# A hybrid decoder step on one core: v projected ahead of the sample requests' attention, layer norm of the gate moved between the samples

## The reference

```python
h = rmsnorm(x, norm_mix)
q_b, k_b, v_b, z_u, z_v, q_c, gate_logits = split(h @ w_in, IN_SPLITS)
u = gelu(z_u); v = layernorm(gelu(z_v), ln_v_g, ln_v_b)
A = u * (W_s v + b)                      # causal 128x128, four channel groups
B = dilated window attention(q_b, k_b, v_b)   # sample rows: keys and values of a cache plus their own
C = attention(q_c, memory)               # sample rows: a cached memory
x = x + (sig(g_A)*P_A(A) + sig(g_B)*P_B(B) + sig(g_C)*P_C(C)) @ w_out
x = x + MoE(rmsnorm(x))                  # top 4 of 32 experts, clamped SwiGLU
y = rmsnorm(x)
```

## Time and profile before

| | |
|---|---|
| median of three runs | 1395.66 us (1394.77 to 1399.48) |
| the profiled execution | 1399.48 us, span 1397.70 us |
| TensorE busy | 1324.9 us, 95% of the span |
| VectorE busy | 371.7 us, 27% |
| ScalarE busy | 249.1 us, 18% |
| mean granted TensorE clock | 0.984 of full |
| chain that ended last | TensorE 59%, DMA 35%, VectorE 3% |

### The profile page before, as it was taken

One profiled execution on the slowest core, in us unless ns is written; L12 is line 12 of the kernel. 1 busy time (PEld: TensorE's weight loads), 2 busy tenths in 40 slices (PEclk: granted clock), 3 DMA queues, 4 the chain that ended last, 5 costly groups with the idle time before them and its releaser, 6 DMA issues.

```text
span 1397.7 us, 19052 instructions
## 1 busy us (share of the span) xinstructions
PE 1324.9 (95%) x7749; PEld 634.9 (45%) x7749; DVE 371.7 (27%) x832; ACT 249.1 (18%) x406; POOL 60.2 (4%) x101
## 2 busy tenths in 40 slices
PE   6999889969996999999999999999999999999997
PEld 5675477637753333433343333333334333343333
DVE  2105654211316222212221222212222122221223
ACT  2011122210214211111121112111111111121112
POOL 2031401110000000000000000000000000000000
PEclk9999999989998999999999999999999999999999
DMA  9998876477873899999999999999999999999994
GB/s 339 374 347 300 281 261 218 158 228 269 314 318 139 310 430 429 429 429 429 428 429 428 428 429 429 429 428 430 429 428 428 428 429 430 428 429 429 429 427 174
DMA packets 56939, 515.13 MB, mean 369 GB/s; under 512 B 5379, under 2 KB 6491, under 8 KB 31536
## 3 DMA queue, kind: packets, MB, share of 16 engines
q1 hardware_dynamic: 50000, 493.68, 86.0%
q0 software_dynamic: 6576, 20.25, 4.5%
q10 hardware_dynamic: 336, 0.82, 0.2%
HBM read 511.21 MB, written 47.52 MB: 400 GB/s over the span
## 4 chain that ended last, share of the span: by engine, by line
PE 59%; DMA 35%; DVE 3%; issue 1%; ACT 1%; POOL 0%; SPq 0%; DVEq 0%; ACTq 0%
PE psum L567 56%; DMA weights<-in_w_gate_up 34%; PE psum L570 2%; DMA weights<-in_w_mem_kv 1%; DMA weights<-in_cache_mem_kv 1%; DVE qk L1387 1%; DVE pair L1233 0%; ACT th L1556 0%; DVE x L1415 0%; POOL weights L510 0%; DVE kvt L1279 0%; DVE kc L1292 0%; DVE va L1110 0%; DVE va L1111 0%; DVE va L1109 0%
## 5 line engine op out<-in xcount | busy, mean ns | idle before, releaser
L567 PE MATMUL psum<-weights,wsp 128*64 128x512 f32 x2048 | 487.5, 602 | 12.4 <-DMA weights<-in_w_gate_up 11.1
L567 PE MATMUL psum<-weights,merged 128*64 128x512 f32 (+2 forms) x1152 | 272.8, 595 | 1.5 <-issue 1.5
L567 PEld LDWEIGHTS psum<-weights,wsp 128*64 128x64 f32 x2048 | 129.3, 136 | 255.5 <-issue 202.6
L1358 DVE TENSOR_TENSOR hT<-psum,hT 128x264 f32<-128x264 f32 x256 | 98.8, 428 | 515.0 <-PE psum L567 515.0
L567 PE MATMUL psum<-hT,weights 128*128 128x264 f32 x704 | 164.3, 391 | 1.2 <-DVE pair L1233 0.9
L567 PEld LDWEIGHTS psum<-weights,merged 128*64 128x64 f32 (+2 forms) x1152 | 89.6, 140 | 156.3 <-issue 154.6
L567 PEld LDWEIGHTS psum<-hT,weights 128*128 128x128 f32 x704 | 133.7, 192 | 28.6 <-DVE pair L1233 4.6
L1617 ACT COPY bT<-psum 128x264 f32<-128x264 f32 x33 | 12.5, 380 | 476.6 <-PE psum L570 476.5
L567 PE MATMUL psum<-bT,merged 64*128 64x264 f32 x512 | 91.6, 435 | 0.0
L1387 DVE TENSOR_SCALAR qk<-psum,lowest 128x512 f32<-128x512 f32 x64 | 48.0, 751 | 158.3 <-PE psum L567 154.8
L567 PEld LDWEIGHTS psum<-bT,merged 64*128 64x128 f32 x512 | 38.5, 184 | 103.8 <-issue 103.8
(11 more groups left out here) (270 smaller groups left out, 727.4 us busy)
## 6 DMA issues: line engine op xcount, KB each, us to landing
weights<-in_w_gate_up SPq DMA_DIRECT2D x128, 2048.0 KB, 24.6
weights<-in_w_down SPq DMA_DIRECT2D x64, 2048.0 KB, 22.9
out<-in_cache_win_kv SPq DMA_DIRECT2D x8, 4094.0 KB, 20.7
weights<-in_w_in SPq DMA_DIRECT2D x13, 2048.0 KB, 12.4
out<-in_cache_win_kv SPq DMA_DIRECT2D x2, 4088.0 KB, 19.4
weights<-in_cache_mem_kv POOLq DMA_DIRECT2D x14, 512.0 KB, 7.4
weights<-in_cache_win_kv POOLq DMA_DIRECT2D x42, 128.0 KB, 5.7
weights<-in_w_mem_kv SPq DMA_DIRECT2D x2, 2048.0 KB, 17.8
```

What stands on the lines that cost most here:

```text
L567: return nc.tensor.matmul(out, lhsT, rhs, start=start, stop=stop, **kw)
L1358: V.tensor_tensor(acc[:, c, :], p_a[j % 2][part], acc[:, c, :], ALU.add).then_inc(s_acc, 1)
```

## The change

In the list, all of v (prompt and samples) is projected right after k, then come all six kt, then qc. zv 0 moves between qcs and qrest, vts ahead of qlow. Between the samples stand now zvs, zv 1, zvz and the four zu. norm_v moves from behind sdot 6 to behind sdot 3; vat and sp come ahead of sdot 6. The weight blocks of v are loaded ahead of qc's, with `LAST_USE` to match. On POOL the twelve outputs of keys and values are issued ahead of keys(3) instead of behind keys(7).

```diff
-    out += [("qc", cols(w_in, CO, CO + 512)), ("v0", cols(w_in, VO, VO + 512)), ("v1", cols(w_in, VO + 512, VO + 768))]
-    out += [("zv", cols(w_in, ZO, ZO + 512)), ("zu", cols(w_in, UO, UO + 512))]
+    out += [("v0", cols(w_in, VO, VO + 512)), ("v1", cols(w_in, VO + 512, VO + 768))]
+    out += [("qc", cols(w_in, CO, CO + 512)), ("zv", cols(w_in, ZO, ZO + 512)), ("zu", cols(w_in, UO, UO + 512))]
...
-    s += [("kt", 2, 0), ("kt", 2, 1)] + [("qc", m) for m in range(4)]
-    s += [("qs", 0), ("qs", 1), ("qcs",), ("vs", 0), ("qrest",), ("v", 0, 0), ("qlow",), ("kt", 0, 0), ("kt", 0, 1), ("selfb",)]
-    s += [("skb", 0), ("skc", 0), ("skb", 1), ("kt", 1, 0), ("kt", 1, 1), ("vsz", 0)]
-    fill = {2: [("v", 1, 0)], 3: [("vs", 1), ("v", 0, 1)], 4: [("vsz", 1), ("v", 1, 1)], 5: [("zv", 0)], 6: [("zvs",), ("vts",)], 7: [("zv", 1)]}
+    s += [("vs", 0), ("v", 0, 0), ("vsz", 0), ("v", 1, 0), ("vs", 1), ("v", 0, 1), ("vsz", 1), ("v", 1, 1)]
+    s += [("kt", t, n) for t in range(3) for n in range(2)] + [("qc", m) for m in range(4)]
+    s += [("qs", 0), ("qs", 1), ("qcs",), ("zv", 0), ("qrest",), ("vts",), ("qlow",), ("selfb",)]
+    big = [("zvs",), ("zv", 1), ("zvz",)] + [("zu", m) for m in range(4)]
+    s += [("skb", 0), ("skc", 0), ("skb", 1)]
     for b in range(2, NS):
-        s += fill[b] + [("skc", b - 1), ("skb", b), ("sdot", b - 2)]
-    s += [("zvz",), ("zu", 0), ("zu", 1), ("sdot", NS - 2), ("norm_v",), ("skc", NS - 1), ("zu", 2), ("zu", 3), ("vat",)]
-    s += [("sp", 0), ("sp", 1), ("sp", 2), ("sp", 3), ("sdot", NS - 1), ("p", "a", 0), ("g", "a", 0), ("slog",)]
+        s += {2: big[0:2], 3: big[2:4], 7: []}.get(b, big[b:b + 1]) + [("skc", b - 1), ("skb", b), ("sdot", b - 2)]
+        if b == 5:
+            s += [("norm_v",)]
+    s += [("vat",), ("sp", 0), ("sp", 1), ("sp", 2), ("sp", 3), ("sdot", NS - 2), ("p", "a", 0), ("skc", NS - 1), ("sdot", NS - 1), ("g", "a", 0), ("slog",)]
...
-LAST_USE = {("kc", 3): 0, ("vc", 1): 1, ("q", 3): 2, ("k", 1): 3, ("k", 5): 4, ("qc", 3): 5, ("v", 1, 0): 6, ("v", 1, 1): 7,
+LAST_USE = {("kc", 3): 0, ("vc", 1): 1, ("q", 3): 2, ("k", 1): 3, ("k", 5): 4, ("v", 1, 0): 5, ("v", 1, 1): 6, ("qc", 3): 7,
...
-            for b in range(KEYS, NS):
-                keys(b)
             taken(pool, "v", 1, 1)
             taken(pool, "vsz", 0)
             taken(pool, "vsz", 1)
-            taken(pool, "kt", 1, 1)
+            taken(pool, "kt", 2, 1)
...
+            for b in range(KEYS, NS):
+                keys(b)
             for b in range(ROUND):
                 values(b)
```

## The result

The changed kernel takes **1409.68 us** (median of 4 runs, 1407.23 to 1411.33), the kernel before beside it 1396.02 (1394.77 to 1399.48): ratio 1.0092, 95% interval 1.007 to 1.0113. The forecast was 1407.5, with 1401 to 1413 as range. The profiled execution took 1409.84 us, its span is 1408.0.

A forecast was written before the change was run, and what follows sets the result against it. It took the mixer ahead of the DMA-bound experts to pass delays one for one, with VectorE's list setting the changed stretch: 9.0 us of waits plus 2.9 of clock, 11.9 on the median 1395.66, gives 1407.5; range 1401 to 1413.

The forecast's parts named there:

- step 6: Clock loss behind new TensorE waits: 1.7 us at zvs and zv 1, 0.5 at skb 7 and vat, 0.7 at "p" and "g".
- Steps 1 and 2: TensorE up to skb 0: eight groups move ahead, done at 150.9, then a 2.6 us wait to 153.5.
- step 2: ScalarE waits for zv 0's Gelu before casting q, then VectorE's qlow; TensorE idles 2.6 us ahead of skb 0.
- Step 3: sdot 0 to 3: skc 1 behind zvs and zv 1 makes sdot 2 2.9 us later, zvz and a zu 0.6.
- The signs to watch for: Expected after: TensorE waits of 2 to 3, some 8 and 4 us, VectorE without long gaps 154 to 209, score at 211 to 215.
- Steps 4 and 5: Layer norm behind sdot 3 takes 9.9 us, TensorE waits some 8, then 4 more; second score 9.0 later before clock loss.
- (a): Rival: TensorE is the limit, its waits and clock loss go, 11.6 us faster, 1384.1; chance 0.06.
- Step 7: POOL and SP: moved outputs, key landings and weight blocks cost nothing, with 3 us as bound for late keys.
- (b): Rival: no change, as the DMA-bound expert stage makes up a late mixer, 1395 to 1398; chance 0.05.
- (c): Rival: smaller delay of 3 to 8 us (no clock loss at skb 0, better overlap, slack given back), 1399 to 1404; chance 0.10.
- (d): Rival: larger delay of 15 to 20 us, from late key streams or more clock loss, 1411 to 1416; chance 0.11.
- The term of 0.6: Layer norm's root: by the Trainium skill's drain of about 1.38 us per table switch, the sum would be 0.6 us higher.

The follow-up runs named there:

- e1: Changed kernel with the casts of q (qrest) ahead of zv 0 in the list, so ahead of its Gelu on ScalarE: 1406.15 us, ratio 1.0089.
- e2: Changed kernel with the layer norm back behind sdot 6, skc 7 ahead of it and the gate behind it: 1410.33 us, ratio 1.0118.
- e9: Changed kernel with the last reduction of sdot 4 to 7 done twice, 5.0 us more VectorE work: 1415.23 us, ratio 1.0147.
- e3: Changed kernel with POOL's old order, keys 3 to 7 ahead of the twelve outputs: 1408.2 us, ratio 1.01.
- e4: Changed kernel with both reductions of each sdot cut to an eighth of their columns (most score terms left out): 1407.44 us, ratio 1.0088.
- e8: e6 with vs 1, and vsz 1 behind it, one place later: 1389.46 us, ratio 0.9957.
- e7: e4 with the four cache shifts behind the ring on SP each put off by one weight block: 1404.11 us, ratio 1.0062.
- e6: Kernel before with zv and zu ahead of v's second half, layer norm behind sdot 2, ring reordered, outputs behind POOL's maximum: 1387.7 us, ratio 0.9939.
- e10: Kernel before with the last reduction of sdot 0 to 3 done twice, the same 5.0 us of VectorE: 1396.14 us, ratio 0.9997.

## Why the prediction was right, step by step

Times are from the start of the changed part (99.63 before, 96.46 after), so that the 3.17 us of the two executions don't enter.

| step | forecast, us | measured, us |
|---|---|---|
| 1 and 2: start to skb 0 | 53.9, of it 2.6 of wait | 54.3, of it 2.74 |
| 3: skb 0 to the start of the norm, with step 6's 1.7 | 24.2 | 24.4 |
| 4: layer norm | 9.9 | 10.1 |
| TensorE's wait for it | some 8 | 8.63 |
| its wait ahead of skc 6 | 4 | 3.36 |
| 5: gate, from the end of sdot 5 to the start of sdot 6 | 4.8 (and 0.5 in step 6) | 5.9 |
| 5: sdot 7 to the second score | 7.2 | 7.2 |
| second score later by, steps 1 to 6 | 11.9 | 12.5, and 1.4 behind it |

**Steps 1 and 2** hold within half a microsecond. Eight groups that stood between the samples now stand ahead of skb 0, and ScalarE's list adds its wait. e1 shows the second part: without zv 0 ahead of the casts 1.13 of the 2.74 go and, with them, the fall of the clock. In the changed kernel the Gelu of zv 0 is what ends last, as step 2 has it. But vts ahead of qlow in VectorE's list stands 1.13 us behind it as a second bound, which step 2 doesn't name; that is why e1 won less than expected.

**Step 3** holds: VectorE waits 4.77 us for TensorE in sdot 1 and 0.68 in sdot 2, and from then on no more than 0.6 at a time. The signs to watch for asked for no long gap from 154 on; the 4.77 is the one that step 3 had itself (2.9, and 1.7 for the clock).

**Steps 4 and 5** carry the result. The step's claim was that what stands between two sdots in VectorE's list stands between two skc too. The wait of 8.63 shows it, e2 shows that it doesn't hang on the norm's place, and e9 that work added to that list comes out at the second score, 4.0 of 5.0 us, as far as it doesn't fill the gate's idle time. For the root the profile has 0.33 us of idle time where 4.51 stood. The term that was mis-sized is the gate: from the end of sdot 5 (194.51) to the start of sdot 6 (200.37) it took 5.9, as VectorE idles 0.59 and 0.41 us for vat and "sp", which lie in the stretch of half clock.

**Step 6** had the right sign and was too small. Its 1.7 at zvs and zv 1 measured 1.65 (10.64 against 8.99 in e1). Its other 1.2 (0.5 at skb 7 and vat, 0.7 at "p" and "g") stand against 1.1 more in the gate and 1.4 behind the second score. The 0.7 fell in another place than forecast: "p" at the gate was slow (3.50 instead of 1.94) without holding VectorE up, and the 1.7 at a later "g" shows in some executions and not in others, in kernels of both orders. Its bound of 3.4 was read too high: it takes the clock of 20 us that hold the idle 3.60 as well. The rows behind that wait give 1.25 for 0.71 and 9.07 for 7.03 (the earlier trace rows and the timeline of before), 2.6 us in all, so the 11.6 of rival (a) was 0.8 too much.

**Step 7** came out at nothing, as e3 shows, but the reason given is only half right. The issue order costs nothing measurable; the landing of sample 7's keys, worst case 11.4 us, took 12.5, and its cover was down to 2 us. e4 ran into it as soon as VectorE was quicker.

**The rivals.** (a), TensorE as the limit, is refuted: its waits grew from 8.5 us (3.60, 1.08, 2.87 and 0.91) to 18.7 with its work unchanged. It was the rival that the Trainium skill spoke for, "Perfetto Trace Analysis", Identifying the Most-Contended Engine, which would have the engine of the highest occupancy improved first; for TensorE it adds that matmul busy time is no good measure of how close to roofline it is. By occupancy TensorE was busy 89% of the stretch (67.98 of 76.45 us) and VectorE 67%; the runs show the pace with the engine that is less busy. (b), the delay made up by the experts, is refuted by 941.86 against 942.30. (c), 3 to 8 us, didn't come: the clock did fall behind skb 0, and even e1, where it doesn't, is 10.8 us slower than the kernel before. (d) didn't come: the keys landed in time, by 2 us.

The other rule weighed was the drain behind a table load. Timeline of ScalarE, changed kernel:

```profile
176.29 1.28 ACT L1526 ACT_TABLE_LOAD   x1
178.62 0.20 ACT L1526 ACTIVATE stat<-stat 128x3 f32<-128x3 f32 x1 [1.05 <-DVEq L1105]
```

The load ends at 177.57, the statistics at 178.53, and the root starts 0.09 behind them. The Trainium skill, "ScalarE: Activation LUTs", What ACT_TABLE_LOAD costs, would have the drain last until 178.95; this trace doesn't show it. Nor does ScalarE's timeline of the kernel before, where the load ends at 180.61 and the root starts at 180.62. The term of 0.6 stays out of the sum.

**What stays open.** Why e8's 1.9 us at the second score don't reach the median; where most of the difference between e4 and e7 comes from; how much of the last 1.4 us behind the second score is the change's doing; and what added work in sdot 4 to 7 would cost in the kernel before.

## What to carry to other kernels

When two engines hand work back and forth, each in its own fixed order, write down the second engine's list between two hand-overs and add it up: work taken out from between them leaves the first engine with nothing to wait beside, whatever the busy shares say. Work that covers another engine's chain has to come after the chain starts, so move what starts the chain forward (zv here) and keep the rest as cover, as e6 does. Before counting on a shortened list, look at the next bound behind it: here the keys stood 2 us away and "g" behind those.

## What the runs showed of the hardware

- The clock stays down when the engine is busy only now and then: in the changed kernel TensorE did 9.42 us of work between 182 and 203 at a granted clock of 0.52 of full, the 1.2 GHz level nearly throughout.
- The length of a wait alone doesn't say whether the clock falls behind it. Behind the wait of 2.74 us zvs and zv 1 took 10.64 us, and behind 1.61 in e1 they took 8.99. But the wait of 2.2 us that every version has in its attention was followed by a "g" at full clock in five of the thirteen profiles and by one of 4.91 to 5.41 us in eight. TensorE, kernel before and then e10, whose programs are the same there:

```profile
227.77 0.70 PE L567 MATMUL psum<-kc,qcT 128*128 128x256 f32 x2 [2.21 <-ACT weights L1536]
228.31 3.72 PE L567 MATMUL psum<-hT,weights 128*128 128x264 f32 x16
...
226.89 0.70 PE L567 MATMUL psum<-kc,qcT 128*128 128x256 f32 x2 [2.20 <-ACT weights L1538]
227.43 5.41 PE L567 MATMUL psum<-hT,weights 128*128 128x264 f32 x16
```

- A 512 KB load that lands 5.1 us after its issue takes 12.5 to 15.0 when it is issued while a 4 MB copy from a cache to its output is under way on SP's queue (issued at 180.39 in the changed kernel, 19.8 us to land). With that copy moved in e7 the same load took 5.0, and the wait of 3.88 us was gone. The price isn't fixed: in e6 two such loads beside the copy took 8.3 and 8.4 us, and the copy itself 30.1.
